# Each engine of two attention stages walks its own order of the woven events, with running minima and key halves copied by ScalarE

## The reference, cut to what matters

```python
z = rmsnorm(x) @ w_in                        # columns: q rank | kv latent | rope key | dq | dk | dv
# (A) latent attention, 8 heads
#   prompt: causal softmax over 1024 keys of (q_nope.k_nope + q_rope.kr) * 96**-0.5, times v
#   sample: the query is carried into the latent (128), scores against 2048 paged latents + own 8
# (B) dilated window attention, 8 heads of 64
#   prompt: three windows (128,1), (512,4), (2048,16), merged by their softmax denominators
#   sample: the same windows over 2048 saved keys and values + own 8
h = x + concat(A, B) @ w_out
y = h + (silu(causal_conv3(rmsnorm(h) @ w_gate)) * (rmsnorm(h) @ w_up)) @ w_down
out = rmsnorm(y)                             # and the new caches
```

## Time and profile before

| | |
|---|---|
| median of three runs | 1998.89 us (1998.84 to 1999.7) |
| profiled execution, its own time | 1998.15 us |
| its span, first to last instruction | 1996.6 us |
| busy: PE, PEld | 1777.9 us (89%), 1549.3 us (78%) |
| busy: DVE, ACT, POOL | 896.7 us (45%), 652.3 us (33%), 571.5 us (29%) |
| mean granted TensorE clock | 0.941 of full speed |

### The profile page before, as it was taken

One profiled execution on the slowest core, in us unless ns is written; L12 is line 12 of the kernel. 1 busy time (PEld: TensorE's weight loads), 2 busy tenths in 40 slices (PEclk: granted clock), 3 DMA queues, 4 the chain that ended last, 5 costly groups with the idle time before them and its releaser, 6 DMA issues. The chain is left out here.

```text
span 1996.6 us, 27887 instructions
## 1 busy us (share of the span) xinstructions
PE 1777.9 (89%) x9955; PEld 1549.3 (78%) x9955; DVE 896.7 (45%) x1858; ACT 652.3 (33%) x1321; POOL 571.5 (29%) x533
## 2 busy tenths in 40 slices
PE   3999968888996878886969969999999999999997
PEld 2888857777875766776757859889889888888885
DVE  5333325566664666565743412332332333333335
ACT  4222115556554544544432212112211211211212
POOL 0000003554552446564630012212212311321211
PEclk9999988899987988998979979999999999999999
DMA  7222133233106553543334127488578659668632
GB/s 237 102 101 92 70 98 87 57 89 89 45 6 160 145 155 94 162 114 110 92 128 153 27 78 144 117 156 127 129 138 135 137 121 161 123 126 177 107 74 94
DMA packets 156106, 227.41 MB, mean 114 GB/s; under 512 B 31111, under 2 KB 129032, under 8 KB 149576
## 3 DMA queue, kind: packets, MB, share of 16 engines
q1 hardware_dynamic: 153134, 159.39, 26.8%
q0 software_dynamic: 2880, 66.85, 20.7%
HBM read 201.12 MB, written 91.93 MB: 147 GB/s over the span
## 5 line engine op out<-in xcount | busy, mean ns | idle before, releaser
L2168 DVE TENSOR_TENSOR acc<-f_dp,acc 128x512 f32<-128x512 f32 x198 | 136.5, 691 | 197.9 <-PE f_dp L2249 197.9
L2039 POOL TENSOR_TENSOR f_gl<-f_graw,f_gh 128x1024 fp32r<-128x1024 f32 x22 | 52.9, 2404 | 378.8 <-ACT f_gh L2083 378.8
L2249 PE MATMUL f_dp<-f_dh,f_ah 128*128 128x512 f32 x396 | 155.4, 392 | 4.6 <-DVE f_al L2199 4.0
L2249 PE MATMUL f_dp<-f_dl,f_ah 128*128 128x512 f32 x396 | 154.9, 391 | 0.0
L2249 PE MATMUL f_dp<-f_dh,f_al 128*128 128x512 f32 x396 | 154.7, 391 | 0.0
L2182 DVE SCALAR_TENSOR_TENSOR f_gc<-f_gp,f_coef,f_gc 128x832 f32<-128x832 f32 x44 | 47.7, 1085 | 233.4 <-ACT f_lasts L2103 230.5
L523 PE MATMUL zp<-win_h,xT_h 128*128 128x512 f32 (+1 forms) x288 | 112.7, 391 | 0.0
L1550 POOL TENSOR_TENSOR w_vl<-w_v,w_vh 96x2048 fp32r<-96x2048 f32 (+3 forms) x32 | 111.2, 3486 | 2.0
L523 PE MATMUL zp<-win_l,xT_h 128*128 128x512 f32 (+1 forms) x288 | 111.4, 387 | 0.0
L523 PE MATMUL zp<-win_h,xT_l 128*128 128x512 f32 (+1 forms) x288 | 111.3, 386 | 0.0
L768 POOL TENSOR_SCALAR l_pr<-l_pr,l_rden 128x128 f32<-128x128 f32 (+7 forms) x64 | 47.0, 746 | 172.1 <-DVE l_rden L868 172.1
(11 more groups left out here) (343 smaller groups left out, 4886.6 us busy)
## 6 DMA issues: line engine op xcount, KB each, us to landing
out_s_win_k<-in_state_win_k POOLq DMA_DIRECT2D x10, 3264.0 KB, 43.5
out_s_win_v<-in_state_win_v POOLq DMA_DIRECT2D x10, 3264.0 KB, 46.0
w_k<-in_state_win_k SPq DMA_DIRECT2D x16, 768.0 KB, 7.2
w_v<-in_state_win_v SPq DMA_DIRECT2D x16, 768.0 KB, 5.6
f_graw<-in_w_gate SPq DMA_DIRECT2D x22, 512.0 KB, 4.4
f_uraw<-in_w_up SPq DMA_DIRECT2D x22, 512.0 KB, 4.9
f_draw<-in_w_down SPq DMA_DIRECT2D x11, 1024.0 KB, 34.5
m_c<-in_cache_kv_latent SPq DMA_DIRECT2D x128, 64.0 KB, 1.8
```

The lines of the kernel that those rows point to most:

```text
L2039: nc.gpsimd.tensor_tensor(w_lo[n][:], w_raw[n][:], w_hi[n][:].bitcast(F32), ALU.subtract)\
L2168: nc.vector.tensor_tensor(a, dp[h][:], a, ALU.add).then_inc(S["d_add"], 1)
L2249: last = nc.tensor.matmul(dp[h][:], a[:, c, t * P:(t + 1) * P], w[:, c, h * 512:(h + 1) * 512], start=(c == 0 and j == 0), stop=(c == 1 an ...
```

## The change

1. **Minima that run on.** The second chunk's `score` starts its minimum from the first chunk's (a per-partition scalar read from `nm`, in place of the constant HUGE); likewise each `s` from the one before it, the first one from `s_new`, and each window `score` from the one before it. The DVE instructions at L864, L1233 and L1626 go, with the semaphore `min`, and `exp` waits for the last score itself. A DVE wait on the earlier score is added.
2. **Key halves by ScalarE.** The copy of `kh` to `kl` moves from DVE (L837) to a new event `swap` on ACT.
3. **An order for each engine.** `turns_of` sorts the woven list anew for each engine: an event keeps its place plus a number of places from a table, by side (0 prompt, 1 sample) and kind. SP's order stays.
4. **Waits for the new orders.** ACT's copies of `prep`, `cT`, `rT` and `k_turn` wait for the products that still read the tile they write over, since TensorE may now transpose before them. `Ring.plan` numbers banks by TensorE's order and counts releases by ACT's and DVE's.
5. In A, `rT` goes from ahead of `cT` to behind `rows` in the plan.

```diff
+        used = {eng: [(e, sides[i].bank_use(e)) for i, e in turns[eng] if sides[i].bank_use(e)]
+                for eng in ("tensor", "scalar", "vector")}
+        self.by = [e for e, _ in used["tensor"]]
+        self.use = {e: u for u, e in enumerate(self.by)}
...
 # PromptSide
+            if self.kind == 1 and what == 1:
+                E.append((("swap", n, f), 0))
...
+            if n:
+                last = n * PT - 1
+                self.ring.ready(act, ("score", last - 4, 1, 0) if what == 0 and f == 0 else ("score", last, 1, f))
...
+        elif e[0] == "swap":
+            _, n, f = e
+            cols = slice(f * 512, f * 512 + 512)
+            self.ring.done(act, ("prep", n, 1, 0, f))
+            nc.scalar.copy(self.kl[0:HD, :, cols], self.kh[HD:P, :, cols]).then_inc(S["k_ok"], 1)
...
-                if last:
-                    act.wait_ge(S["min"], k // PT * 4 + s - 3)
-                else:
-                    self.ring.done(act, ("score", k, h, 0))
+                self.ring.done(act, ("score", k, h, last))
...
-            if what == 1:
-                self.ring.done(dve, e)
-                nc.vector.tensor_copy(lo[0:HD, :, cols], hi[HD:P, :, cols]).then_inc(S["k_ok"], 1)
...
+            low = HUGE
+            if c:
+                self.ring.done(dve, ("score", k, h, 0))
+                low = self.nm[:, k % 2, 0, h:h + 1]
...
-                m = self.nm[:, k % 2]
-                nc.vector.tensor_tensor(m[:, 2, :], m[:, 0, :], m[:, 1, :], ALU.min).then_inc(S["min"], 1)
...
 # LatentSide
-                E.append((("rT", g), 0.45))
                 E.append((("cT", g), 0.45))
...
+            if b < B:
+                if g + 1 < 4 * B:
+                    E.append((("rows", g + 1), 0))
+                E.append((("rT", g), 0.45))
...
+            if k == "s":
+                self.ring.done(dve, ("s", e[1] - 1) if h else ("s_new", b))
+                low, at = self.st[rows, h:h + 1], h + 1
...
-            nc.vector.tensor_reduce(self.st[rows, 5:6], self.st[rows, 0:5], AX.X, ALU.min).then_inc(S["min"], 1)
...
+def turns_of(order, later):
+
+    return {eng: [x for _, x in sorted(((n + later.get(eng, {}).get((x[0], x[1][0]), 0), x) for n, x in enumerate(order)),
+                                       key=lambda at: at[0])]
+            for eng in ("sync", "gpsimd", "scalar", "vector", "tensor")}
+
+
+LATENT_LATER = {
+    "gpsimd": {(0, "over"): 8, (0, "split_v"): 11},
+    "scalar": {(0, "exp"): 1, (0, "out"): 4, (0, "prep"): -1, (0, "turn"): -2, (1, "cT"): 2, (1, "exp"): 5,
+        (1, "final"): 8, (1, "p"): -1, (1, "pre_qr"): 8, (1, "pre_uk"): -3, (1, "setup"): 5},
+    "vector": {(0, "out"): -1, (0, "prep"): 1, (0, "score"): -1, (1, "cT"): 4, (1, "fold"): 3, (1, "p"): 1,
+        (1, "s"): 2, (1, "s_new"): 1, (1, "setup"): 9},
+    "tensor": {(0, "prep"): -1, (0, "turn"): -2, (1, "cT"): 2, (1, "final"): 5, (1, "fold"): 1, (1, "o"): -1,
+        (1, "p"): 3},
+}
+
+
+DILATED_LATER = {
+    "gpsimd": {(1, "v_split"): -15},
+    "scalar": {(0, "exp"): 3, (0, "out"): 4, (0, "prep"): -3, (0, "swap"): 5, (1, "exp"): 3, (1, "fold"): 2,
+        (1, "k_turn"): -1, (1, "q_block"): -4},
+    "vector": {(0, "over"): -3, (0, "score"): -1, (1, "pre"): 3, (1, "score"): 1, (1, "value"): 2},
+    "tensor": {(0, "prep"): -5, (0, "turn"): -2, (0, "value"): 2, (1, "k_turn"): -1, (1, "score"): 1},
+}
...
-        order = weave(sides, ((0, 1), (0.09, 0.97)))
-        ring.plan(order, sides)
+        turns = turns_of(weave(sides, ((0, 1), (0.09, 0.97))), LATENT_LATER)
+        ring.plan(turns, sides)
...
-            for i, e in order:
+            for i, e in turns["scalar"]:
                 sides[i].scalar(act, e)
...
 # WindowSide
+            if g >= 2:
+                act.wait_ge(S["s_ps"], g - 1)
             nc.scalar.copy(self.kT_h[g % 2][:, 0:w], bank[:, 0:w]).then_inc(R["bank_hi"], 1)
...
-            nc.vector.tensor_reduce(self.st[rows, 3:4], self.st[rows, 0:3], AX.X, ALU.min).then_inc(S["min"], 1)
```

More of the change, by code:

```diff
@@ L1149, in scalar @@
             b = e[1]
-            act.wait_ge(S["min"], b + 1)
+            self.ring.done(act, ("s", 4 * b + 3))
             p = self.pr[self.half(b), :]
-            nc.scalar.activation(p, p, ACT.Exp, bias=self.st[self.half(b), 5:6], scale=-1.0,
+            nc.scalar.activation(p, p, ACT.Exp, bias=self.st[self.half(b), 4:5], scale=-1.0,
                                  accum_out=self.st[self.half(b), 6:7]).then_inc(S["exp"], 1)
@@ L1224, in vector @@
                 self.ring.ready(dve, ("p", b - 2, 1))
+            low, at = HUGE, 0
+            if k == "s":
+                self.ring.done(dve, ("s", e[1] - 1) if h else ("s_new", b))
+                low, at = self.st[rows, h:h + 1], h + 1
             dve.sem_inc(S["neg_go"])
[L1226 to L1232, removed]
-            nc.vector.tensor_reduce(self.st[rows, 5:6], self.st[rows, 0:5], AX.X, ALU.min).then_inc(S["min"], 1)
+            nc.vector.tensor_tensor_reduce(out=self.pr[rows, cols], in0=src, in1=tab, scale=-MLA_SCALE, scalar=low,
+                                           op0=ALU.add, op1=ALU.min, accum_out=self.st[rows, at:at + 1]).then_inc(R["bank_d"], 1)
         elif k == "p":
@@ L1398, in _ @@
         def _(sp):
-            for i, e in order:
+            for i, e in turns["sync"]:
                 sides[i].sync(sp, e)
@@ L1405, in _ @@
         def _(pool):
-            for i, e in order:
+            for i, e in turns["gpsimd"]:
                 sides[i].gpsimd(pool, e)
@@ L1415, in _ @@
         def _(dve):
-            for i, e in order:
+            for i, e in turns["vector"]:
                 sides[i].vector(dve, e)
@@ L1420, in _ @@
         def _(pe):
-            for i, e in order:
+            for i, e in turns["tensor"]:
                 sides[i].tensor(pe, e)
@@ L1617, in vector @@
                 self.ring.ready(dve, ("p_turn", b - 2, 1))
+            low = HUGE
+            if u:
+                dve.wait_ge(S["s_free"], 3 * b + u)
+                low = self.st[rows, u - 1:u]
             dve.sem_inc(S["neg_go"])
```

56 lines of the change are left out of this document (19 added, 37 removed).

## The result

The median is 1863.11 us (1861.05 to 1867.36), against 1998.87 before (the three executions above and a fourth): ratio 0.9323, 95% interval 0.9306 to 0.934.

What follows compares the result with a forecast made beforehand. Latent and dilated stages were taken as bound by PE's work plus its queue waits, with low clock adding. From 1998.15 us, 49 us of waits and 20 of clock gave 1929, median 1930, range 1905 to 1955 (chance 0.54).

Steps and rivals of the forecast that it cites:

- Swap and minima: Dilated stage: key-half copy moved to ACT saves 13.3 us of waits, removing DVE's minimum instructions saves 10 us.
- Orders: New engine orders cut TensorE's waits: 8 and 5.6 us in the dilated stage, 8.5 and 4 us in the latent one.
- of the other 16 I take half: Dilated stage, window keys: of 22.2 us of waits about 6 go with the minima; of the other 16, 8 saved.
- the value splits: Dilated stage: POOL's splits go 15 places forward, ending half of TensorE's 11.2 us of waits, 5.6 us.
- the rope rows: Latent stage: later `over` on POOL and `rT` on PE end half of 16.9 us of waits, 8.5 us.
- first keys: Start of the latent stage: ACT's `setup` five places back lets scores go first, saving 4 us of 9.3.
- the 20 us: Latent and dilated stages: low-clock loss of 75 us falls by 20 as waits go; slow starts stay (bounds 0 and 27).
- all of it: Rival: every term at its upper bound, 86 us of waits, clock part capped at some 25 us: 1887 us, chance 0.12.
- Only the held instructions: Rival: swap and minima save 23.3 us of waits and 12.6 of clock, orders nothing: 1962 us, chance 0.20.
- Splits in front of the normalisation: Rival: on POOL, 15 earlier value splits delay normalisations that PE's transposes need, 98 us: 2028 us, chance 0.06.
- The scalar is held: Rival: dilated-stage scores reading an SBUF scalar are held by POOL's splits, 23 us on DVE: 1950 us, chance 0.05.
- Nothing moves: Rival: new ACT waits take the place of the old ones: 1998 us, chance 0.03.

Runs made afterwards that it cites:

- e1: Changed kernel with both order tables empty and `rT` ahead of `cT` again; running minima and ScalarE swap stay: 1946.8 us, ratio 0.9746 to the kernel before.
- e4: Changed kernel with only the key-half swap back on DVE: 1878.9 us, ratio 0.9408 to the kernel before.
- e3: Changed kernel with only the three DVE minimum instructions back in place of the running minima: 1887.6 us, ratio 0.9452 to the kernel before.
- e2: Changed kernel with the order tables and moved `rT` kept, but DVE minimum instructions back and the swap on DVE: 1900.2 us, ratio 0.9518 to the kernel before.
- e9: Changed kernel with `rT` ahead of `cT` again and, in the dilated stage, without ScalarE's later prompt `exp`: 1872.5 us, ratio 0.9368 to the kernel before.
- e6: Changed kernel without ScalarE's entries in both order tables: 1895.0 us, ratio 0.9472 to the kernel before.
- e7: Changed kernel without TensorE's entries in both order tables: 1900.5 us, ratio 0.9502 to the kernel before.
- e8: Changed kernel without VectorE's (DVE's) entries in both order tables: 1881.1 us, ratio 0.9409 to the kernel before.
- e5: Changed kernel without GpSimd's entries in both order tables: 1880.0 us, ratio 0.9406 to the kernel before.
- e13: Changed kernel with ScalarE repeating the swap of the third pair's first half 2 more times, as a stall: 1872.1 us, ratio 0.9373 to the kernel before.
- e14: Changed kernel with ScalarE repeating the swap of the third pair's first half 4 more times, as a stall: 1870.8 us, ratio 0.937 to the kernel before.
- e15: Changed kernel with ScalarE repeating the swap of the third pair's first half 9 more times, as a stall: 1876.6 us, ratio 0.9394 to the kernel before.

## Why the prediction was wrong

The direction was right, and so was the mechanism of the held DVE instructions; the sizes of two terms were not, and some gains came at other waits, or by other entries, than those named.

**Swap and minima: right in sum, in part by luck.** 23.3 us of idle time were forecast in the dilated stage, e1 shows 25.7; taken back alone they cost 11.9 (minima, forecast 10) and 9.4 us of idle time (swap, forecast 13.3). The swap on ScalarE took 1.046 us, forecast 1.03. But the swap was argued from TensorE's wait for the key halves, which fell by 5.4 us in e1 and comes back by 0.9 in e4; most of what e4 loses stands at the subtraction behind the copy, where the prediction has DVE going "straight on". And the window keys' wait fell by 13.0 us in e1, where about 6 were put into the minima. Missed: the minima in the latent stage, counted as nothing, cost it some 7 us in e3, 3.2 of them idle time.

**Orders: the step that failed is "of the other 16 I take half", and so on for the value splits and the rope rows.** Forecast 8 + 5.6 + 8.5 + 4 = 26.1 us of idle time; the tables alone took 62.1 (e2), and 53.6 on top of e1. Two parts of it can be told apart. The named waits (window keys, key halves, value splits, rope rows, first keys) fell by 67.6 us in all, from 82.8 to 15.2, not by 49.4; the halves stood for ScalarE's new waits and had no row behind them. For the window keys the new wait is there:

```profile
ACT w_kth L1599 <- PE w_s_ps L1708: 7.1, 8, 2.1
```

It is 7.1 us on ScalarE, and TensorE waits 0.8 us in all for what follows. The other 16.9 us are waits that the sum did not name: L937 for L872 in the dilated stage (13.7 us, now 4.7) and its smaller fellows. The wait of L937 is 10.8 us in e1 and 11.6 in e2 and e4, so it takes swap and tables together; the smaller ones were not tried by themselves.

The causes named for two of the waits do not hold as they stand either. The window keys' was laid above all to the exponentials ahead of ScalarE's key copies, but it stays short without the later exponentials (e9, 2.1 us) or without ScalarE's whole table (e6, 3.3), and comes back without TensorE's (e7, 7.0). The first keys' was laid to ScalarE's `setup` alone, but DVE's entry is needed as much (e8). And the sum had no new wait for a load, where 4.2 and 2.6 us came.

**Clock: the step that failed is the 20 us, and the "some 25" that capped the rival "all of it".** Of the 28.8 us by which 20 was too low, some 20 follow from the idle time forecast too small (35.1 us at 0.58), the rest from the discount for the starts. The prediction held that the starts would keep their slow clock, and they do. Windows of the changed kernel for the start and the rest of each stage:

```profile
273.00:305.00 32.00, 19.55 (x98) 17.50 (x99) 11.45 (x30) 12.37 (x34) 6.08 (x9) 0.63 0.50 129
305.00:566.90 261.90, 251.19 (x1826) 225.12 (x1824) 181.56 (x507) 169.71 (x376) 149.79 (x223) 0.99 0.27 71
566.90:600.00 33.10, 15.56 (x73) 13.27 (x74) 12.85 (x36) 18.09 (x46) 9.13 (x14) 0.64 0.90 225
600.00:895.40 295.40, 282.03 (x1933) 250.61 (x1932) 203.21 (x518) 185.70 (x421) 211.98 (x128) 0.98 0.54 153
```

and of the kernel before:

```profile
273.00:312.00 39.00, 21.24 (x102) 19.29 (x103) 12.13 (x32) 13.32 (x36) 6.03 (x9) 0.61 0.44 114
312.00:615.00 303.00, 269.43 (x1822) 237.91 (x1821) 183.82 (x528) 167.79 (x375) 148.54 (x223) 0.93 0.23 60
615.00:645.00 30.00, 13.84 (x60) 11.36 (x61) 13.67 (x35) 15.01 (x41) 8.39 (x12) 0.60 0.89 229
645.00:1031.50 386.50, 315.36 (x1945) 275.96 (x1945) 235.51 (x551) 181.28 (x418) 211.82 (x128) 0.89 0.42 119
```

Before, the starts held 8 + 6 of the clock's part by their rows (0.39 x 21.2 and 0.40 x 13.8), and the rest of the two stages 19 + 35 = 54; after, the rest holds 0.01 x 251 + 0.02 x 282 = 8. So some 45 us of the clock's part lay where waits could be removed, and nearly all came back. The cap of 25 was not read from any window. In proportion to idle time (49.4 of 138.6) the 20 would have been 27; with the 84.5 us that went it is 46, and 48.8 were measured.

**The rivals.** "All of it" came nearest: its 86 us of waits against 84.5 measured, and only its cap on the clock kept it at 1887. That the two agree so closely is luck: its 86 counted 32.9 us of DVE's busy time in place of waits, and of the 84.5 us, 16.9 came from waits that nobody had named. "Only the held instructions" fell by e2. "Splits in front of the normalisation" did not come: TensorE waits 0.7 us once for L764 in the dilated stage (and 0.9 once in the latent one), and without the earlier splits (e5) the stage is 14 us longer. "The scalar is held" did not come either: the scores with it differ by some 60 ns from those without (below). "Nothing moves" fell with the result. Of the signs set out beforehand, no DVE instruction of the dilated stage is above 0.8 us, and the clock reached 0.95 instead of 0.92. One sign of being wrong did come: the longest chained scores last 746 ns in the mean, above the 0.7 us set. That limit was badly chosen, since the same scores with the constant take 683 ns and L1646 already took 749 with such a scalar.

## What to carry to other kernels

When a wait has an event standing in front of it that an edit moves away, a discount on it needs a row of its own; here 67.6 of 82.8 us of named waits went. Ask too which waits without a name stand behind the same engine, and find by single removals which entry ends a wait before giving it the credit. Split the clock's part by place, start of a stage against the rest, before capping it: what is lost between scattered waits comes back with them, here at 0.58 us for each us of idle time in the whole change (0.57 in e1, 0.68 in e2), though for a single stall that did not hold. Tables for several engines work together: taken away one at a time they cost 104 us in sum, taken away together (with `rT`'s move, e1) 84.

## What the runs showed of the hardware

The scalar that a DVE score reads from SBUF costs some 60 ns and is not held. The scores with the constant and with the scalar, in the dilated stage of the changed kernel (busy us, mean ns | idle before):

```profile
L856 DVE CUSTOM_DVE_ANT_0 l_pr<-l_bank,l_table 128x512 f32<-128x512 f32 x40 | 26.8, 683 | 1.8 <-PE l_bank L906 1.8
...
L856 DVE CUSTOM_DVE_ANT_0 l_pr<-l_bank,l_table,l_nm 128x512 f32<-128x512 f32 x8 | 6.0, 746 | 2.3 <-PE l_bank L906 2.3
...
L856 DVE CUSTOM_DVE_ANT_0 l_pr<-l_bank,l_table,l_nm 128x384 f32<-128x384 f32 x8 | 4.7, 612 | 0.0
...
L856 DVE CUSTOM_DVE_ANT_0 l_pr<-l_bank,l_table 128x384 f32<-128x384 f32 x8 | 4.2, 550 | 0.0
```

The difference is 63 and 62 ns; over the 48 scores of the stage that is 3 us of DVE time, while GpSimd's L1573 is busy for 111.7 us beside them. The Trainium skill, SBUF — State Buffer, section Who interferes with whom, says that a DVE instruction with at most one SBUF input, outside the two-port modes, does not contend with GpSimd. The stage's longest score with the scalar, 757 ns, agrees, with the scalar not counting as a second input.

After the stall of 2.3 us in e13, TensorE was busy without a gap and yet at the low level (1.2 of 2.4 GHz) for 5.6 us, to about 732. By windows of 1 us it was 3.8 us after the 4.4 us of e14, 3.5 us after the 9.8 us of e15, and 8.5 us after the 8.7 us at 906 of the kernel before. Windows of 4 us of e13, behind the stall's end at 726.7:

```profile
728.00:732.00 4.00, 4.00 (x16) 3.22 (x14) 1.53 (x4) 1.92 (x4) 0.37 (x1) 0.50 0.66 211
732.00:736.00 4.00, 4.00 (x34) 4.00 (x33) 1.57 (x5) 1.36 (x5) 0.00 (x0) 0.97 0.14 55
```

and of e15, around the stall's end at 734.1:

```profile
724.00:734.00 10.00, 0.28 (x2) 0.00 (x0) 0.92 (x2) 9.69 (x11) 4.26 (x1) 0.67 0.35 121
734.00:738.00 4.00, 3.91 (x12) 3.18 (x13) 1.76 (x5) 2.87 (x7) 0.00 (x0) 0.55 0.02 4
738.00:742.00 4.00, 4.00 (x37) 4.00 (x35) 1.76 (x5) 1.73 (x6) 0.00 (x0) 1.00 0.00 0
```

A longer stall was not always dearer in the clock.
